# Pool in place of ScalarE issues the late modulation transfers, and the gate transposes stand two tiles later

## The reference

```python
mod_l = (silu(c) @ ada_w[layer] + ada_b[layer]).reshape(batch, 1, N_MOD, D_MODEL)      # 6 x 1024 numbers
mod_c = (silu(c_ctx) @ ada_w[layer] + ada_b[layer]).reshape(1, 1, N_MOD, D_MODEL)
h_l = rms_norm(x, norm1_g) * (1 + mod_l[:, :, 1]) + mod_l[:, :, 0]
h_c = ...                                                                             # the same with mod_c
qa, ka, va, oa, ga, qb, kb, vb = split(h @ w_in)                                      # for h_c and h_l
gates = (g[0], log_sigmoid(g[1]), g[2], log_sigmoid(g[3]))                            # g = ga + gate_b, 4 heads
qb, kb = rms_norm(qb, q_norm_g), rms_norm(kb, k_norm_g)                               # then rope on the latent part
ha = mlstm(qa, ka, va, gates)         # running sums and maxima of the gates along the tokens
ob = attention(qb, kb, vb)
x = x + mod_l[:, :, 2] * (concat(ha, ob) @ w_out)
x = x + mod_l[:, :, 5] * (relu(modulate(x, mod_l, 3, 4) @ w1) ** 2 @ w2)
```

## Time and profile before

| | us |
|---|---|
| median of 3 runs | 4193.43 |
| lowest and highest run | 4183.21, 4193.45 |
| the profiled execution | 4185.72 |
| its span from first to last instruction | 4183.9 |
| PE busy in the span | 3884.3 (93%) |
| DVE busy | 2113.2 (51%) |
| ACT busy | 1318.8 (32%) |
| POOL busy | 0.2 (4 instructions) |

### The profile page before, as it was taken

How to read it: one execution, slowest core, us unless ns; L and a number is a source line. 1 busy time by engine, 2 the same in 40 slices (tenths; PEclk the granted TensorE clock), 3 DMA queues, 4 the chain that set the end, 5 groups by cost and what they waited for, 6 DMA issues and landing times.

```text
span 4183.9 us, 44583 instructions
## 1 busy us (share of the span) xinstructions
PE 3884.3 (93%) x18548; PEld 3168.6 (76%) x18548; DVE 2113.2 (51%) x3672; ACT 1318.8 (32%) x2004; POOL 0.2 (0%) x4
## 2 busy tenths in 40 slices
PE   7887999999999999999999787999999997779998
PEld 5885479999986688888878555888788876467886
DVE  5644667654456543343365465533633473836335
ACT  4423434222256432222233313322322244123222
POOL 0000000000000000000000000000000000000000
PEclk9899799999999999999999758999999998579999
DMA  6320003343310122232222001222222221002222
GB/s 217 96 86 1 1 31 104 124 129 126 109 66 26 45 96 96 96 114 96 96 86 96 31 1 41 87 100 96 88 96 96 96 86 61 1 15 82 97 100 81
DMA packets 103116, 333.34 MB, mean 80 GB/s; under 512 B 11362, under 2 KB 11522, under 8 KB 102660
## 3 DMA queue, kind: packets, MB, share of 16 engines
q1 hardware_dynamic: 77040, 278.10, 19.3%
q10 hardware_dynamic: 25876, 52.39, 4.0%
HBM read 328.35 MB, written 2.10 MB: 79 GB/s over the span
## 4 chain that ended last, share of the span: by engine, by line
PE 87%; DVE 8%; ACT 4%; issue 1%; DVEq 0%; DMA 0%; ACTq 0%; SPq 0%
PE PS L505 70%; PE PS L1070 2%; PE PS L507 2%; PE PS L1055 1%; PE PS L1086 1%; PE PS L1058 1%; PE PS L1416 1%; PE PS L1387 1%; DVE scratch L556 1%; PE PS L2030 0%; PE PS L1782 0%; PE PS L1783 0%; PE PS L936 0%; ACT arena L990 0%; PE PS L2033 0%
## 5 line engine op out<-in xcount | busy, mean ns | idle before, releaser
L505 PE MATMUL PS<-arena_r,ring_hi 128*128 128x512 f32 (+1 forms) x6224 | 2106.8, 377 | 97.0 <-DVE H_r L672 95.6
L505 PE MATMUL PS<-arena_r,ring_r 128*128 128x512 f32 (+1 forms) x4752 | 1783.6, 375 | 0.0
L505 PEld LDWEIGHTS PS<-arena_r,ring_hi 128*128 128x128 f32 x6224 | 1170.8, 189 | 279.3 <-DVE H_r L672 60.8
L505 PE MATMUL PS<-H_r,ring_hi 128*128 128x512 f32 (+1 forms) x3280 | 1234.3, 376 | 0.0
L505 PEld LDWEIGHTS PS<-arena_r,ring_r 128*128 128x128 f32 x4752 | 899.8, 189 | 131.5
L374 DVE TENSOR_TENSOR ring_r<-ring,ring_hi 128x1024 fp32r<-128x1024 f32 x514 | 627.7, 1222 | 671.9 <-ACT ring_hi L365 671.3
L365 ACT ACTIVATE ring_hi<-ring 128x1024 fp32r<-128x1024 f32 x514 | 541.8, 1055 | 914.0 <-DMA ring<-weights_dram 847.1
L505 PEld LDWEIGHTS PS<-H_r,ring_hi 128*128 128x128 f32 x3280 | 625.3, 191 | 95.3 <-issue 2.4
L1645 ACT ACTIVATE arena<-PS 128x512 f32<-128x512 f32 x88 | 52.6, 598 | 532.0 <-PE PS L505 532.0
L1224 DVE SCALAR_TENSOR_TENSOR XH<-PS,mods,XH 128x256 f32<-128x256 f32 (+1 forms) x144 | 68.6, 524 | 234.1 <-PE PS L505 234.1
L336 DVE CAST arena_r<-arena 128x512 fp32r<-128x512 f32 (+1 forms) x184 | 74.3, 404 | 200.1 <-ACT arena L1270 197.0
(11 more groups left out here) (349 smaller groups left out, 3109.4 us busy)
## 6 DMA issues: line engine op xcount, KB each, us to landing
ring<-weights_dram SPq DMA_DIRECT2D x526, 512.0 KB, 3.2
rstd<-ada_later_dram ACTq DMA_DIRECT2D x54, 256.0 KB, 2.7
mean<-ada_later_dram ACTq DMA_DIRECT2D x53, 256.0 KB, 2.8
ada_extra<-ada_later_dram ACTq DMA_DIRECT2D x53, 256.0 KB, 2.9
XH<-xT_dram ACTq DMA_DIRECT2D x1, 3072.0 KB, 19.7
ring<-weights_dram ACTq DMA_DIRECT2D x4, 512.0 KB, 4.1
out_dram<-XH SPq DMA_DIRECT2D x8, 256.0 KB, 2.0
con<-second_dram ACTq DMA_DIRECT2D x1, 1536.0 KB
```

Source lines behind the costliest of these rows:

```text
L505: ins = pe.matmul(PS[:, o.bank, 0:hi - lo], w[:, 0, :], x, **flags)
```

## The change

`ada_fetch` no longer stands in ACT's program. It is the whole program of POOL: a loop over the 160 halves, in which each transfer waits only until its slot is used up. Two further waits keep the first of them from the slots that hold the roots of the norms: before half 0 for the 16 scaled pieces of the first norm, before half 48 for those of the second. The second edit puts `gates_pe` behind tile 15 instead of tile 13.

```diff
-        def ada_fetch(act, n):
-
-            if n >= ADA_SLOTS:
-                act.wait_ge(ada_used.sem, n - ADA_SLOTS + 1)
-            act.dma_start(ada_slot(n)[:], ada_d[n]).then_inc(ada_loaded[n % ADA_SLOTS].sem, 16)
+        def ada_fetch(pool):
+
+            for n in range(2 * len(ADA_LATER)):
+                if n == 0:
+                    pool.wait_ge(affine_done.sem, KD * len(ALL))
+                if n == 48:
+                    pool.wait_ge(affine_done.sem, 2 * KD * len(ALL))
+                if n >= ADA_SLOTS:
+                    pool.wait_ge(ada_used.sem, n - ADA_SLOTS + 1)
+                pool.dma_start(ada_slot(n)[:], ada_d[n]).then_inc(ada_loaded[n % ADA_SLOTS].sem, 16)
...
             for i, n in enumerate(halves):
-                tiles[i // per].setdefault("ada_load", []).append(n)
                 tiles[i // per + 1].setdefault("ada_sum", []).append(n)
...
                     high_up_to(eng, t["last_slab"] + 3)
-                    for n in t.get("ada_load", []):
-                        ada_fetch(eng, n)
                     if "beside_act" in t:
...
-            t[13]["beside_pe"] = gates_pe
+            t[15]["beside_pe"] = gates_pe
...
+        @block.gpsimd
+        def _(pool):
+            ada_fetch(pool)
+
```

## The result

The changed kernel takes 4143.31 us (median of 4 runs, 4140.04 to 4144.0) against 4192.62 us of the kernel before in the same series: a ratio of 0.9889, 95% interval 0.9877 to 0.9901. That is faster by 1.1%, clear of the 0.3% that can be told from no change. The profiled execution took 4143.77 us, its span 4142.0 us, 41.9 us shorter than before. Where the kernel before was run more often beside the experiments, its median was 4188.2 us (19 runs), 4185.6 us (13 runs) and 4182.9 us (7 runs), so that the gain is better put at 40 to 49 us.

The account below looks back on a forecast made before the run. PE, 87% of the chain, was held to lose 37 us in the projection stage to waits on ACT and DVE and slow clock; 4189 (mean of four runs) - 37 = 4152 us, range 4134 to 4174.

Parts of the forecast that it names:

- The bound and the ring of waits: Projection stage: ACT's root waits behind transfers needing DVE's sums, DVE waits for ACT; PE waits 20.6 us at head sums.
- The sum for PE: Projection stage, 164.0 us against 126.8 us of PE work: 37 us lost, 26.6 of waits and some 10.6 of slow clock.
- The schedule tile by tile: Projection stage: DVE's and PE's times per tile; no PE wait from tile 5 on, tile 17 ending at 213.7 us.
- The landing on POOL: Time from slot used to half landed when POOL issues: taken as 4.5 us, bounds 3.3 and 6.7 us.
- The sign that was to confirm 4.5 us: DVE waits for `rstd` of 0.5 to 1 us in tiles 2 to 4 would show that landing time.
- The skill's warning about a DVE operation beside transfers from POOL: POOL cannot write descriptors during DVE's two-port modes: landing 5.8 us, gain 34 us; an estimate the forecast did not use.
- The gate transposes: Behind tile 13 PE would wait 1.5 us, costing 3 us with slow clock; behind tile 15 nothing, at no cost.
- Elsewhere: Outside the projection stage no gain: its last two tiles only move, and feed-forward PE is already busy 100.00 of 100 us.
- (a): Rival: POOL's landing is slow; gain 31 us at 6.7, 25 at 8, 9 at 10; chance 0.06 for 7 to 9 us.
- (b): Rival: only issue time is gained, 16 us of idle ACT's issues, time stays 4189; shares 0.06 for no change.
- (c): Rival: POOL's issuing holds DVE up, lengthening its tile; with 5.5 us more per tile, slower, about 4213; chance 0.04.
- (d): Rival: ACT still waits for DVE's sums in the projection stage; given next to nothing, within the 0.06 for no change.

Follow-up runs that it names:

- experiment 1: Changed kernel, but ACT again waits at the old places until the halves are used up, issuing nothing; POOL still issues all 160 transfers: 4169.73 us.
- experiment 5: Kernel before, but ACT issues a tile's three transfers behind its copies, not ahead of its root; gate transposes behind tile 15: 4151.68 us.
- experiment 3: Changed kernel with the gate transposes back behind tile 13, so only POOL's issuing is new against the kernel before: 4143.92 us.
- experiment 6: Kernel before, but POOL issues halves 0 to 47 (projection stage), ACT the other 112; gate transposes behind tile 15: 4143.48 us.
- experiment 7: Kernel before, but POOL issues halves 48 to 159 (feed-forward stage), ACT the first 48; gate transposes behind tile 13: 4181.65 us.
- experiment 8: Changed kernel, but POOL asks for half n of the first 48 only when half n-2 is used up, not n-3: 4159.54 us.
- experiment 9: Changed kernel, but POOL asks for half n of the first 48 only when half n-1 is used up, not n-3: 4249.47 us.
- experiment 2: Kernel before with only the gate transposes moved from behind tile 13 to behind tile 15, ACT issuing as before: 4184.08 us.

## Why the prediction was right

**The bound and the ring of waits.** Right. Experiments 1 and 5 show it from both sides: waits without issues bring the loss back, issues behind the copies mostly do not.

**The sum for PE, 37 us.** The stage gave 38.6 us. The term was a little small because two pieces of PE's work were priced too high: a tile with head sums takes 9.71 us from copy to copy in the changed kernel (tile 4 at 96.65, tile 5 at 106.36), so the head sums cost 1.28 us and not 1.45, five times; and from 194.49 to 204.00 the tile with the transposes takes 9.51, so they cost 1.1 us and not 1.5. That is 1.3 of the 1.6 us. The schedule tile by tile, which the 37 us rest on, put tile 17 at 213.7; its copy came at 212.4. Run again with a landing of 3.35 us, the schedule also held when DVE was made late: 229 against a measured 229.8, and 300 against 299.3.

**The landing on POOL, 4.5 us.** Wrong in size: 3.3 us, which is the lower end of the range given. DVE waited 0.3 to 1.5 us three times in the stage (2.7 us in all), in place of 0.6 us and more in every short turn. For PE nothing hung on it, since DVE had a lead in either case. The sign that was to confirm 4.5 us, a wait for `rstd` of 0.5 to 1 us in tiles 2 to 4, did appear (0.92 us in tile 2, at half 3's first use) and was misleading. The schedule has a split ahead of tile 2's sums; in both traces they follow tile 1's directly, so that DVE waits there at 3.3 us as well, and did so for 0.69 us before.

**The skill's warning about a DVE operation beside transfers from POOL.** By the prediction's estimate from the page of the Trainium skill ("SBUF — State Buffer", section "Summary: rules for kernel authors"; the two times stand in its section "A bandwidth-pool intuition that's wrong (but worth ruling out)"), asking to landing would have taken about 5.8 us. Half 3 took 3.32 us from asking to use, and the landing alone was 3.0 us in the median and 5.2 at most, with DVE busy for 38.95 of 40 us [second of the 40 us stretches above]. So the delay did not appear. This is no test of the page's case: in this stage DVE runs only eight one-input casts (L336, from 64 to 72 us), and none while a transfer is issued. In the feed-forward stage it runs 78 of them, of about 0.36 us each, and the landing there was 3.0 us in the median and 4.7 at most.

**The gate transposes.** The step that failed. The prediction said that the transposes behind tile 13 would wait 1.5 us and cost 3 us beside the first edit. That followed from the landing of 4.5 us, by which the closing sum ends at 180.6. With 3.3 us it ended at 177.2 in experiment 3, 1.0 us before PE asked. The landing accounts for some 2.5 of the 3.4 us (an estimate: the same schedule with 3.35 us); the rest is that DVE's turns are a little shorter than priced, 10.5 us and not 10.6 in tiles 4 to 8. The second edit is free, and worth nothing here.

**Elsewhere.** Right for the feed-forward stage (experiments 6 and 7), where PE is still busy for all of the time:

```profile
900.00:950.00 50.00, 50.00 (x287) 50.00 (x286) 25.06 (x54) 17.24 (x30) 6.46 (x12) 1.00 0.39 127
```

It left out that the stage in between moves with the clock.

**The number.** Forecast 4152, measured 4143.3, within the range. The 8.7 us are: 1.6 us of the stage (mostly the two prices above), 3.3 us behind the stage (2.4 of it slow clock in the attention stage), and 3.3 us because the forecast was set against a mean of 4189 and not against the profiled execution of 4185.7, which sums up to 8.2 us; the rest is between one run and the median.

**The rivals.** (a) is out: the landing is 3.3 us. Its prices for 6.7, 8 and 10 us were not run themselves; the schedule that gave them held in experiments 8 and 9, where the request was late instead. (b), the gain as issue time, is refuted by experiment 1. The Trainium skill's "DMA: Bandwidth & Descriptors", section "Issuing engines are not separate DMA queues", gives another issuer only the time of issuing. No run contradicts that as far as issuing goes: POOL's issuing was worth 1.6 us in the stage while ACT still waited (experiments 1 and 2). The gain came from the wait ahead of an issue. (c) is out: the sums take 0.69 us as before, and DVE's turn is 103.79 - 93.30 = 10.5 us with six sums. (d) is out: from 58 to 260 us ACT waits for PE, for slabs and at the next stage's start, and never for a sum (L561).

## What to carry to other kernels

A transfer that is issued from a computing engine costs that engine the wait for its slot, and not only the 0.33 us of the issue: look at what stands behind it in program order before moving anything, since issuing a few lines later may give most of the gain. When two engines are each half idle and yet a third waits for both, write down their turns with durations from the trace; the sum of a turn against the pace of the third engine says whether the ring or an engine is the bound, and how late a transfer may be. And judge an edit of a few microseconds by where its own stage ends in the trace, since other stages can move the total by more.

## What was not expected of the hardware

**Issue time and packets.** An issue takes 538 ns on POOL, where it counts as busy, and 334 ns on ACT. The first one took 672 ns. From asking to first use half 3 took 3.3 us with either; from issue to landing the median is 3.0 us on POOL and 2.7 us on ACT. POOL's queue moved its part in fewer packets: in the page of the changed kernel the 160 transfers (41.95 MB) are 12,800 packets; the ACT queue had 25,876 packets before and has 2,836 now, so the same bytes were 23,040 packets there.

```profile
q0 software_dynamic: 12800, 41.95, 3.3%
q10 hardware_dynamic: 2836, 10.44, 0.7%
```

They took 3.3% of the engines' span in place of 3.3% (4.0% less 0.7%): the number of packets made no difference to that share.

**The clock.** The same 1280 products of the attention stage ran at a mean granted clock between 0.85 and 0.90 from trace to trace, and the stage took between 344.8 and 360.5 us with it. These 15.6 us are about a third of the gain of this change.
